# Gated delta net in a two-layer backbone: diagonal blocks of 8 by substitution on VectorE, doubling on TensorE from 8, and the loop around them reordered

## The reference

```
decay = exp(where(causal, gcum[i] - gcum[j], -inf))
m     = where(strict, (k_beta @ k.T) * decay, 0)
sol   = triangular_solve(eye + m, [v*beta, k_beta*exp(gcum)])
attn  = (q @ k.T) * decay
# scan over the chunks, per head, with the state S:
v_new = u - w @ S
o     = q_dec @ S + attn @ v_new
S     = S * exp(g_last) + k_dec.T @ v_new
```

## Time and profile before

| what | value |
|---|---|
| time, median of 3 runs | 1365.07 us (1364.43 to 1365.12) |
| profiled execution, first to last instruction | 1368.2 us |
| PE busy, share of the span | 1344.0 us, 98% |
| DVE busy | 861.3 us, 63% |
| ACT busy | 698.0 us, 51% |
| POOL busy | 288.0 us, 21% |
| the loop over the 8 steps (first L3003 to last state product) | about 345.6 to 571.4 us |

### The profile page before, as it was taken

How to read it: one execution, slowest core, us unless ns; L and a number is a source line. 1 busy time by engine, 2 the same in 40 slices (tenths; PEclk the granted TensorE clock), 3 DMA queues, 4 the chain that set the end, 5 groups by cost and what they waited for, 6 DMA issues and landing times.

```text
span 1368.2 us, 27958 instructions
## 1 busy us (share of the span) xinstructions
PE 1344.0 (98%) x11250; PEld 1269.2 (93%) x11250; DVE 861.3 (63%) x1324; ACT 698.0 (51%) x1123; POOL 288.0 (21%) x296
## 2 busy tenths in 40 slices
PE   6999999999999999999999999999999999999998
PEld 3899999998899999899999999999999988999998
DVE  4654789985456565542587665666746766865663
ACT  4358888878544455422543312343126655664543
POOL 2000223322566787531100000000020000200002
PEclk8999999999999999999999999999999999999999
DMA  9722232321411110123455566555423221556562
GB/s 324 205 78 85 86 87 84 87 85 63 140 47 32 55 40 32 63 74 105 139 185 188 182 194 193 189 194 185 139 90 127 94 73 37 174 181 210 181 192 79
DMA packets 138032, 170.91 MB, mean 125 GB/s; under 512 B 10912, under 2 KB 121760, under 8 KB 137920
## 3 DMA queue, kind: packets, MB, share of 16 engines
q1 hardware_dynamic: 137312, 169.13, 38.7%
q0 software_dynamic: 608, 0.19, 0.1%
HBM read 168.25 MB, written 1.05 MB: 124 GB/s over the span
## 4 chain that ended last, share of the span: by engine, by line
PE 82%; DVE 7%; ACT 4%; issue 2%; POOL 2%; DMA 1%; SPq 0%; DVEq 0%; ACTq 0%; POOLq 0%
PE bank L2601 54%; PE bank L2609 5%; PE bank L3015 3%; PE bank L3003 3%; DVE w_lo L1686 2%; DVE qkv L1772 2%; PE bank L2527 1%; PE bank L3032 1%; ACT w_hi L919 1%; POOL qkv L772 1%; PE bank L3260 1%; PE bank L2957 1%; PE bank L3283 1%; PE bank L2981 1%; PE bank L2879 1%
## 5 line engine op out<-in xcount | busy, mean ns | idle before, releaser
L1686 DVE TENSOR_TENSOR w_lo<-raw,w_hi 128x1024 fp32r<-128x1024 f32 x212 | 265.0, 1251 | 300.1 <-ACT w_hi L919 299.8
L919 ACT ACTIVATE w_hi<-raw 128x1024 fp32r<-128x1024 f32 x212 | 223.5, 1055 | 379.2 <-PE bank L2601 377.3
L2601 PE MATMUL bank<-h_hi,w_hi 128*128 128x256 f32 x1472 | 300.8, 283 | 5.4 <-DVE w_lo L1686 2.9
L2601 PE MATMUL bank<-h_hi,w_lo 128*128 128x256 f32 x1472 | 293.9, 278 | 0.0
L2601 PE MATMUL bank<-h_lo,w_hi 128*128 128x256 f32 x1472 | 288.3, 278 | 0.0
L2601 PEld LDWEIGHTS bank<-h_hi,w_hi 128*128 128x128 f32 x1472 | 226.4, 189 | 14.9 <-issue 10.6
L2601 PEld LDWEIGHTS bank<-h_hi,w_lo 128*128 128x128 f32 x1472 | 226.0, 189 | 0.0
L2601 PEld LDWEIGHTS bank<-h_lo,w_hi 128*128 128x128 f32 x1472 | 222.8, 189 | 0.3 <-DVE h_lo L1967 0.2
L2601 PE MATMUL bank<-hid_hi,w_hi 128*128 128x256 f32 x768 | 173.0, 280 | 0.0
L2601 PE MATMUL bank<-hid_hi,w_lo 128*128 128x256 f32 x768 | 172.0, 278 | 0.0
L2601 PE MATMUL bank<-hid_lo,w_hi 128*128 128x256 f32 x768 | 171.9, 278 | 0.0
(11 more groups left out here) (370 smaller groups left out, 2532.6 us busy)
## 6 DMA issues: line engine op xcount, KB each, us to landing
raw<-in_mlp_w SPq DMA_DIRECT2D x128, 512.0 KB, 3.6
late_w<-in_w_mod SPq DMA_DIRECT2D x56, 512.0 KB, 4.3
raw<-in_even_w_in SPq DMA_DIRECT2D x48, 512.0 KB, 3.7
raw<-in_w_mod SPq DMA_DIRECT2D x24, 512.0 KB, 4.2
first_w<-in_w_mod SPq DMA_DIRECT2D x16, 512.0 KB, 11.7
raw<-in_even_w_out SPq DMA_DIRECT2D x16, 512.0 KB, 3.4
raw<-in_attn_w_qkv SPq DMA_DIRECT2D x16, 512.0 KB, 3.3
raw<-in_attn_w_o SPq DMA_DIRECT2D x8, 512.0 KB, 3.3
```

The source lines that it names most:

```text
L919: act.activation(stored(w_hi, j, four), raw[:, j % RAW], ACT.Copy).then_inc(hi_ready, 1)
L1686: dve.tensor_tensor(stored(w_lo, j, four), raw[:, j % RAW], stored(w_hi, j, four).bitcast(F32), ALU.subtract).then_inc(split_done, 1)
L2601: return pe.matmul(bank[2 * pair + t][:, c - n0:c - n0 + CTX], w_[:, k, t * P:(t + 1) * P], x_[:, c:c + CTX], start=(kk == 0 and first and ...
```

## The change

The levels become 8, 16, 32 and 64. The inverse of the 8-wide diagonal blocks is now computed by substitution. `neighbours` on DVE masks the system to these blocks, reduces it to 8 numbers a row and spreads them to 64 columns; one PE matmul with the 0/1 matrix `local` gives every partition the 8x8 block it lies in; ACT copies that to `near`. `local` on DVE then runs 7 rounds of a multiply and an add on 8 x k elements, each waiting for the one before. `spread` on POOL writes the result into `d_t`. The first transposed inverse is made by the ordinary chain (level index -1).

Further: `betas` moves from POOL to ACT; `log_gates` of a direction is issued apart and two steps ahead; `rows(q+1)` and `decayed_q` move so that `rows` of the next step are at the end of a step; `d_dt` and `d_qd` get two buffers, `d_raw` and `d_eg` go; the fillers get new places.

```diff
-FILLERS = {0: {3: 2, 4: 3, 5: 3}, 7: {2: 2, 3: 2}}
+FILLERS = {0: {0: 1, 1: 2, 2: 1, 3: 2, 4: 1, 5: 1}, 7: {2: 2, 4: 2}}
...
-        LEVELS = (2, 4, 8, 16, 32, 64)
+        LEVELS = (8, 16, 32, 64)
...
-                pool.tensor_tensor(d_tt[q % 2][:, :, :], d_b[:, :, :], mask("comb"), ALU.mult).then_inc(g_md, 1)
+            def spread(q):
+
+                pool.wait_ge(v_near, 2 * q + 2)
...
                 for d in range(2):
+                    x_ = t_rows[:, d] if d else t_rows[:, d, :, ::-1]
+                    pool.tensor_tensor(d_t[q % 2][:, d].rearrange("p i (b c) -> p i b c", c=LOCAL),
+                                       x_.unsqueeze(2).to_broadcast([P, 4, P // LOCAL, LOCAL]), m_, ALU.mult).then_inc(g_ti, 1)
...
             for q in range(STEPS):
...
+                if q + 2 < STEPS:
+                    log_gates(q + 2, 1)
+                if prep:
+                    spread(q + 1)
...
+            def neighbours(q):
+
+                dve.wait_ge(v_n, q + 1)
+                link(dve.tensor_tensor(d_b[:, :, :], d_n[q % 2][:, :, :], C("local").unsqueeze(1).to_broadcast([P, 4, P]), ALU.mult))
+                link(dve.tensor_reduce(n_rows, d_b[:, :, :].rearrange("p i (b c) -> p i c b", c=LOCAL), mybir.AxisListType.X, ALU.add))
+                dve.tensor_tensor(flat(d_b[:, 0:2]).rearrange("p (i r c) -> p i r c", i=4, r=LOCAL),
+                                  n_rows.unsqueeze(2).to_broadcast([P, 4, LOCAL, LOCAL]),
+                                  place_of.unsqueeze(1).unsqueeze(3).to_broadcast([P, 4, LOCAL, LOCAL]), ALU.mult).then_inc(v_near, 1)
...
+                for k in range(k1, k0, -1):
+                    link(dve.tensor_tensor(t_add[:, :, 0:k], x_[:, :, 0:k, k], t_[:, :, k:k + 1].to_broadcast([P, 8, k]), ALU.mult))
+                    ins = dve.tensor_tensor(t_[:, :, 0:k], t_[:, :, 0:k], t_add[:, :, 0:k], ALU.add)
```

More of the change, by code:

```diff
@@ new lines, in _ @@
+                if q >= 2:
+                    state(q - 2, 1)
+                reduced(q, 0, 0)
+                masked(q, 0, 1)
+                if tail:
+                    rest_of_v(q - 1, 0)
+                masked(q, 1, 0)
+                reduced(q, 0, 1)
+                if prep:
+                    system(q + 1)
+                if tail:
+                    values(q - 1, 0)
+                if prep:
+                    neighbours(q + 1)
+                reduced(q, 1, 0)
+                masked(q, 1, 1)
@@ new lines, in _ @@
+                if q == 0:
+                    split_lo(SEG["out"]["unit"] + 1, 1)
+                scores(q)
+                masked(q, 2, 0)
+                reduced(q, 1, 1)
+                if flip_turn(q):
+                    evac_mod(flip_turn(q))
+                if tail:
+                    state(q - 1, 0)
+                reduced(q, 2, 0)
+                masked(q, 2, 1)
+                if tail:
+                    rest_of_v(q - 1, 1)
+                if prep:
+                    local(q + 1, LOCAL - 1, 4)
@@ new lines, in _ @@
+                if prep and q == 0:
+                    decay(1)
+                if prep:
+                    k_k(q + 1)
+                if tail:
+                    values(t, 0)
+                second_product(q, 1, 0)
+                flip(q, 0, 1)
+                k_q(q)
+                if flip_turn(q):
+                    mod_flip(flip_turn(q))
+                if tail:
+                    out_state(t, 0)
+                mod_filler(mods_in(q, 2))
+                flip(q, 1, 0)
+                second_product(q, 1, 1)
@@ new lines, in _ @@
+                second_product(q, 2, 1)
+                if prep:
+                    rows(q + 1, 1)
+                if tail:
+                    values(t, 1)
+                mod_filler(mods_in(q, 5))
+                second_product(q, 3, 0)
+                flip(q, 2, 1)
+                if prep:
+                    rows(q + 1, 0)
+                mod_filler(mods_in(q, 6))
+                tokens(q, 0)
+                flip(q, LAST, 0)
+                second_product(q, 3, 1)
+                if tail:
+                    out_values(t, 1)
```

485 lines of the change are left out of this document (242 added, 243 removed).

## The result

The changed kernel takes 1396.1 us (median of 4 runs, 1393.4 to 1401.2), the one before 1364.8 (4 runs): a ratio of 1.0225 [1.0202, 1.0248], or 31 us slower. The forecast was 1379, slower by 14, with a range of 1354 to 1389, and the time lies above it. The sign was right, half of the size is missing.

A forecast was written before the change was run, and what follows sets the result against it. The prediction took PE's instructions to bound the loop. To 1365.1 us it added 14.3 for step 0 and 0.2 for steps 1 to 7 (28.2 of waits against 7 x 4.0 saved): 1379.6, said as 1379, range 1354 to 1389.

The forecast's parts named there:

- PE work, 8 steps: Fewer product pairs (3.56 us) and transposes (0.44) on PE: 4.0 us a step, -32.0 in eight steps.
- waits, listed, less those of before: PE's new waits: 28.2 us in steps 1 to 7, 19.5 in step 0, less 1.2 idle there before.
- Work taken off PE pays in full, as long as what replaces it is never late: In the loop PE is busy without a gap, 20.00 of 20 us, so time goes by its instructions.
- start: Step 0, ahead of the first product: `local(0)` ends at 346.6, `spread(0)` at 349.2, so PE idles 3.7 us.
- transfer: Step 0, fourth filler: its tile is requested only after output unit 1 is split, so PE waits 9.7 us.
- second level: `flip(q,1,0)` waits for `reduced(q,1,0)`, now behind `neighbours` on DVE: 2.6 us with even t, 0.85 with odd.
- end of a step: Next step's first product waits for `spread`, which ends 6.2 us after `rows` against 3.0 of cover: 3.3 us.
- step 6: At its end no `log_gates` is left, so the wait for `spread` is 1.35 us.
- the collision: `log_gates` on POOL and `local` on DVE exclude each other, raising the step-end wait from 1.6 to 3.3 us.
- The rival without collisions: Small DVE instructions slip in beside POOL, shortening waits in the second level, step ends and step 0: 1362; chance 0.17.
- More collisions: Rival: first part of `local` and output scaling also meet POOL, 1.3 us more in seven steps: 1389; chance 0.10.
- 1365.1 + 14.3 + 0.2: Old median plus 14.3 us for step 0 and 0.2 for steps 1 to 7: 1379.6, said as 1379.

The follow-up runs named there:

- keep_busy: The changed kernel with unread identity transposes on PE ahead of each of its long loop waits, other engines' orders unchanged: 1381.3 us, 1.011 to the kernel before.
- betas_late: The changed kernel with `betas(q + 2)` moved behind `tokens(q, 0)` on ACT: 1394.0 us, 1.02 to the kernel before.
- spread_first: The changed kernel with `spread(q + 1)` put ahead of `log_gates(q + 2, 1)` on POOL: 1386.3 us, 1.0151 to the kernel before.
- experiment 5: The same run as spread_first: the changed kernel with `spread(q + 1)` ahead of `log_gates(q + 2, 1)` on POOL: 1386.3 us, 1.0151 to the kernel before.
- four_moves: The changed kernel with output unit 1 split early, `spread` ahead of `log_gates`, `betas` and `neighbours` later, first step's `neighbours` copy and half of `local` earlier: 1366.1 us, 0.9989.

## Why the prediction was half right

Account to the first matmul of the output stage, 573.52 before and 600.51 after, so +27.0. (The medians differ by 31; the changed kernel's traced run is 2.7 below its median, and the last 1 to 2 us are in no trace.) The old kernel's waits in the loop, all of them:

```profile
PE bank L2992 <- POOL d_vd L851: 0.5, 1, 0.5
PE bank L3032 <- ACT d_tc L1358: 0.4, 2, 0.2
PE bank L2944 <- DVE d_s L2226: 0.3, 1, 0.3
PE bank L2891 <- POOL d_gl L790: 0.2, 1, 0.2
```

| term | forecast | trace |
|---|---|---|
| PE work, 8 steps | -32.0 | -32.0 by the counts of rows (16 pairs for 24, 8 transposed pairs for 10) |
| waits, listed, less those of before | 28.2 + 19.5 - 1.2 = +46.5 | 43.6 - 1.4 = +42.2 |
| overlap lost, 22 more waits x 0.17 | in the row above | +3.7 |
| matmuls at the lower clock | 0 | the rest, +13.1 |

The rest has a check. The stretches at the lower clock in the changed kernel, summed:

```profile
348.50:355.40 6.90, 5.60 (x20) 4.67 (x20) 0.84 (x2) 2.78 (x7) 4.62 (x5) 0.51 0.00 0
...
sum 37.70, PE 31.29 PEld 28.02 DVE 8.23 ACT 12.82 POOL 19.56; mean PE 3.91 PEld 3.50 DVE 1.03 ACT 1.60 POOL 2.45
```

PE works 31 us of them. Where a pair takes 0.85 for 0.445, that is 15 us lost, an estimate that is somewhat high, as not every instruction takes twice as long. keep_busy's loop, with none of it, is 11.4 us shorter, and its time 14.8.

- *"Work taken off PE pays in full, as long as what replaces it is never late"*: right, and so was the sum of the waits, 46.5 against 45.9, in part because misses cancel. By place: start 3.9 for 3.7; transfer 8.8 for 9.7; second level 9.7 and 6 x 0.17 for 10.4 (2.1, 0.7, 2.1, 1.5, 1.7, 1.5 against 2.6 and 0.85 in turn, too much for the one kind and mostly too little for the other); end of a step 2.03 + 0.97 + 2 x 0.17 = 3.3 for 3.3, step 6 0.7 + 0.7 + 0.3 = 1.7 for 1.35. (The forecast's own terms, 6.2 less 3.0 and 349.2 less 345.6, give 3.2 and 3.6 for its 3.3 and 3.7; nothing hangs on it.)
- *The end's cause* was right in size and half right in kind: `spread` is late for the collision, but two thirds of the wait stand at `tokens`, for an exponential behind `betas` on ACT, which the forecast called cheap. Either cause makes most of the wait by itself: without the `betas` (betas_late) it is 0.69 + 2.29 and two overlaps, 3.3 again, as the forecast has it for `spread` alone, and betas_late gained 2 us at most; without the collision (spread_first) 2.03 are left.
- *The rival without collisions* (1362) is out by 475.93 and 476.98, and by experiment 5. "More collisions", 1389, is nearer to the time than the forecast, but not for its reason: the first part of `local` takes 0.17 to 0.25 us an operation. The output scaling (L2313) did meet POOL, 0.92 us each for 0.58 before, but PE's list has no wait behind it.
- *The step that failed* is the sum itself: "1365.1 + 14.3 + 0.2". It carries PE's prices of the earlier trace rows, taken at a clock of 1.00, over to a loop with 46 us of waits. The clock in the earlier trace rows was read and never used, so the matmuls at the lower clock stood at nothing. The missing term is 13 us by the account and 11 to 15 by keep_busy; with it the forecast would have been 1391 to 1395. A range that allowed for it would have held the time.
- *Step 0* lost most by it: its clock was 0.77 between 345 and 360 and 0.55 between 373 and 380, and the transfer's chain itself came later for it.

## What to carry to other kernels

Where a change turns a gapless TensorE into one that waits, price the matmuls behind the waits at the lower clock too: here isolated waits of 1.0 us cost only themselves (and 0.19 of overlap), 2.0 and 1.0 us with 0.65 of work between them cost 1.4 to 1.6 more in five places of six, 3.7 us cost 1.8 more on average. A wait that can't be removed can be filled, best with work that has to be done anyhow: a filler of 1.0 us moved ahead of a wait gave about 1.0 a step. And look for what stands ahead of a late chain on each engine in turn, since undoing one of two parallel causes only renames the wait.

## What the runs showed of the hardware

- In the changed kernel's trace the same waits of 2.03 and 0.96 us ahead of 514.36 (step 4) left the pairs at 0.445, while at 480.26 and 541.76 they took 0.85 to 0.99. A single wait of 2.12 us lowered the clock behind 402.65 and didn't behind 465.63. Of two like places one lowers the clock and the other doesn't. The four runs of spread_first, alike in everything, spread over 16 us, with mean granted clocks of 0.989 in the fastest and 0.983 in the slowest. That is not all of the spread: the old kernel's runs, all at 0.995 to 0.997, spread over 9. What decides which place it is was not tried.
- Where a strided sum of 512 elements on DVE, the new reduction, was priced like the old contiguous one (0.69), it takes 1.07 to 1.11, in four_moves' step 0 (1.08) with POOL idle. The old one reads PSUM and the new one SBUF; the two differences were not told apart.
- A DVE product of 512 elements beside POOL takes 1.28 to 1.72 us, alone 0.68 (both in four_moves).
